# Down projections of four SwiGLU layers as seven half-size products, in an fp32 decoder trunk on one core

## What is computed

```python
D_MODEL, SEQ, DEPTH, D_FF = 1024, 512, 2, 2816

def swiglu(h, w_gate, w_up, w_down):
    return (jax.nn.silu(h @ w_gate) * (h @ w_up)) @ w_down

for i in range(DEPTH):
    f = swiglu(rmsnorm(x, ffn1_pre_norm[i]), ffn1_w_gate[i], ffn1_w_up[i], ffn1_w_down[i])
    x = x + 0.5 * rmsnorm(f, ffn1_post_norm[i])
    x = x + rmsnorm(mixer_i(rmsnorm(x, mix_pre_norm[i])), mix_post_norm[i])
    f = swiglu(rmsnorm(x, ffn2_pre_norm[i]), ffn2_w_gate[i], ffn2_w_up[i], ffn2_w_down[i])
    x = x + 0.5 * rmsnorm(f, ffn2_post_norm[i])
```

## Time and profile before

| | |
|---|---|
| median of 3 runs | 2147.71 us (2146.5 to 2147.76) |
| span of the profiled execution | 2144.4 us |
| mean granted TensorE clock | 0.999 of full speed |
| PE busy | 2134.5 us, 100% |
| DVE busy | 910.5 us, 42% |
| ACT busy | 745.2 us, 35% |
| moved by DMA | 198.20 MB, mean 92 GB/s |

### The profile page before, as it was taken

One profiled execution on the slowest core, in us unless ns is written; L12 is line 12 of the kernel. 1 busy time (PEld: TensorE's weight loads), 2 busy tenths in 40 slices (PEclk: granted clock), 3 DMA queues, 4 the chain that ended last, 5 costly groups with the idle time before them and its releaser, 6 DMA issues.

```text
span 2144.4 us, 25444 instructions
## 1 busy us (share of the span) xinstructions
PE 2134.5 (100%) x10626; PEld 1793.2 (84%) x10626; DVE 910.5 (42%) x1331; ACT 745.2 (35%) x1167; POOL 75.5 (4%) x79
## 2 busy tenths in 40 slices
PE   9999999999999999999999999999999999999998
PEld 8888888888888888888888888888897679888887
DVE  5333324476666544433322533332255555333322
ACT  5222223444545533422222332222244544222221
POOL 0000000000000000000000000000014100000000
PEclk9999999999999999999999999999999999999999
DMA  5232332222112123423233142333313113323331
GB/s 203 95 94 95 107 99 69 84 93 61 58 60 70 60 79 109 138 98 99 98 99 99 59 138 99 98 99 98 98 58 118 55 64 109 98 99 99 98 99 49
DMA packets 55828, 198.20 MB, mean 92 GB/s; under 512 B 6257, under 2 KB 6897, under 8 KB 55714
## 3 DMA queue, kind: packets, MB, share of 16 engines
q1 hardware_dynamic: 54000, 194.53, 28.3%
q10 hardware_dynamic: 1714, 2.04, 0.3%
HBM read 193.41 MB, written 2.10 MB: 91 GB/s over the span
## 4 chain that ended last, share of the span: by engine, by line
PE 96%; DVE 2%; ACT 1%; issue 1%; DMA 0%; POOL 0%; DVEq 0%; ACTq 0%; POOLq 0%
PE ps L992 18%; PE ps L994 17%; PE ps L993 17%; PE ps L1000 11%; PE ps L1002 11%; PE ps L1001 11%; PE ps L1262 1%; PE ps L1481 1%; PE ps L1510 1%; DVE w_lo L1596 1%; PE ps L1330 1%; PE ps L1019 1%; DVE normed L1602 1%; PE ps L1485 1%; PE ps L1186 1%
## 5 line engine op out<-in xcount | busy, mean ns | idle before, releaser
L992 PE MATMUL ps<-h_hi,w_hi 128*128 128x512 f32 (+1 forms) x1832 | 679.5, 371 | 0.4
L994 PE MATMUL ps<-h_hi,w_lo 128*128 128x512 f32 (+1 forms) x1832 | 674.1, 368 | 0.0
L993 PE MATMUL ps<-h_lo,w_hi 128*128 128x512 f32 (+1 forms) x1832 | 673.7, 368 | 0.0
L509 ACT ACTIVATE w_hi<-raw 128x1024 fp32r<-128x1024 f32 x352 | 370.3, 1057 | 674.0 <-PE ps L994 339.5
L1596 DVE TENSOR_TENSOR w_lo<-raw,w_hi 128x1024 fp32r<-128x1024 f32 x337 | 402.4, 1221 | 331.3 <-ACT w_hi L509 330.6
L992 PEld LDWEIGHTS ps<-h_hi,w_hi 128*128 128x128 f32 x1832 | 345.4, 189 | 59.3 <-issue 1.8
L994 PEld LDWEIGHTS ps<-h_hi,w_lo 128*128 128x128 f32 x1832 | 345.3, 188 | 58.1
L993 PEld LDWEIGHTS ps<-h_lo,w_hi 128*128 128x128 f32 x1832 | 345.5, 189 | 55.9 <-issue 0.2
L1596 DVE TENSOR_TENSOR a_rows<-a_rows,ps 128x512 f32<-128x512 f32 x88 | 60.5, 688 | 614.3 <-PE ps L994 614.3
L1000 PE MATMUL ps<-w_hi,a_hi 128*128 128x512 f32 x704 | 274.4, 390 | 0.0
L1002 PE MATMUL ps<-w_hi,a_lo 128*128 128x512 f32 x704 | 273.9, 389 | 0.0
(11 more groups left out here) (229 smaller groups left out, 1990.2 us busy)
## 6 DMA issues: line engine op xcount, KB each, us to landing
raw<-in_w_gate_up SPq DMA_DIRECT2D x176, 512.0 KB, 3.8
raw<-in_w_down SPq DMA_DIRECT2D x88, 512.0 KB, 3.6
raw<-in_w_vg SPq DMA_DIRECT2D x16, 512.0 KB, 3.6
raw<-in_w_xbc SPq DMA_DIRECT2D x16, 512.0 KB, 3.6
raw<-in_w_even_out SPq DMA_DIRECT2D x16, 512.0 KB, 4.3
raw<-in_w_qk_small SPq DMA_DIRECT2D x9, 512.0 KB, 3.7
raw<-in_w_up SPq DMA_DIRECT2D x9, 512.0 KB, 3.6
raw<-in_w_z SPq DMA_DIRECT2D x8, 512.0 KB, 3.6
```

The lines of the kernel that those rows point to most:

```text
L509: return nc.scalar.activation(to, source, ACT.Copy, scale=scale)
L992: nc.tensor.matmul(to, w_h, hi, start=first, stop=False)
L993: nc.tensor.matmul(to, w_h, lo, start=False, stop=False)
L994: return nc.tensor.matmul(to, w_l, hi, start=False, stop=last)
```

## The change

Each down projection becomes seven products of half the tokens, half the inner rows and half the columns, in the form of Strassen's algorithm with 15 additions. The inner dimension is taken in 11 pairs j of two 128-row tiles: tiles 2j and 2j+1 are the two inner halves, tokens 0 to 255 and 256 to 511 the two token halves, columns 0 to 511 and 512 to 1023 the two column halves. A slot now carries one of the seven (M1 to M7) for one or two pairs j: 42 slots with 6 groups for each M, the last group of one pair only. Each pair and each of two 128-token chunks c is one `token_products`.

- **Activations.** In the gate and up stage DVE makes per pair the four sums s1 to s4. The first three units (a11, s1, s2, for M1, M5, M6) are split on the spot into `a_split`; the other four (a22, a12, s3, s4, for M4, M2, M7, M3) go to DRAM (`spill`) and come back in the down stage (`reload`), where they are split over the first (`REFINED_AFTER`).
- **Weights.** In the gate and up stage ACT's queue loads the four quarters of the pair's down weights (1 MB, `load_job`), DVE forms four sums (`sum_weights`) and ACT's queue stores them (`store_job`). SP later loads them as slots (`load_pair`).
- **Down stage.** The order is `DOWN`; banks are collected in `update` by copies on ACT (e1) and additions on DVE (u2, v, c22, u3, c12, c21, c11), which PE waits for before it uses a bank again (`bank_free`). The steps are placed by hand at slot numbers k.
- **Boundary after a SwiGLU sublayer.** `down_stage` splits no slot of the next sublayer; two splits move into the boundary, and `add_c11` adds M2 for chunks 2 and 3.
- **Elsewhere.** `RAW` is 4.

Of the two functions `down_stage` below, the first is ACT's and the second DVE's; `down` is PE's.

```diff
-RAW = 3
+RAW = 4
...
+PAIRS = FT // 2
+GROUPS = (PAIRS + 1) // 2
+HALF_T = T // 2
...
+def plan_down():
+    order = []
+    for m in range(GROUPS):
+        order += [(name, m) for name in (("M1", "M6", "M5") if m == GROUPS - 1 else ("M6", "M5", "M1"))]
+    for m in range(GROUPS - 2):
+        order += [("M7", m), ("M3", m)]
+    order += [(name, m) for name in ("M7", "M3") for m in (GROUPS - 2, GROUPS - 1)]
+    return order + [("M4", m) for m in range(GROUPS)] + [("M2", m) for m in range(GROUPS)]
...
+BANK = {"M1": 6, "M2": 6, "M6": 2, "M7": 2, "M4": 2, "M5": 4, "M3": 4}
...
+REFINED_AFTER = [min(2 * j + 4, 23) for j in range(PAIRS)]
...
+RELOAD_AFTER = [min(2 * j, 19) for j in range(PAIRS)]
...
+            def store_job(f, j):
+                act.wait_ge(weight_sums, PAIRS * f + j + 1)
+                act.dma_start(sums[f][j], job_rows[j % 2]).then_inc(job_out[j % 2], 16)
...
+            def spill(f, j):
+                act.wait_ge(second_sums, PAIRS * f + j + 1)
+                act.dma_start(spilled[f][j], second_raw).then_inc(spill_out, 16)
...
+            def reload(f, j):
+                act.wait_ge(spill_out, 16 * (PAIRS * f + j + 1))
+                if j >= 4:
+                    act.wait_ge(second_lo, PAIRS * f + j - 3)
+                act.dma_start(back[j % 4], spilled[f][j]).then_inc(back_in[j % 4], 16)
...
+            def down_stage(f, s, n):
...
+                for k in range(C21_AFTER + 1):
+                    if k == E1_AFTER:
+                        act.wait_ge(slot_done, at + E1_AFTER + 1)
+                        for c in range(2):
+                            copy(chunk(update, 2 + c, 0), four(ps[:, BANK["M1"] + c, :])).then_inc(e1_done, 1)
...
+                    while n < stop and slot_before[n] <= at + k:
+                        split_high(n)
+                        n += 1
+                    for j in range(PAIRS):
+                        if k == REFINED_AFTER[j]:
+                            act.wait_ge(back_in[j % 4], 16 * (uses(f, j, 4) + 1))
...
+                            copy(pair(j)[:, 0:4 * HALF_T], back[j % 4]).then_inc(second_hi, 1)
+                    for j in range(PAIRS):
+                        if k == RELOAD_AFTER[j]:
+                            reload(f, j)
...
+            def down(f, s):
...
+                for k, (name, m) in enumerate(DOWN[:tail]):
+                    slot_ready(at + k)
+                    for part in range(min(2, PAIRS - 2 * m)):
...
+                        for c in range(2):
+                            if j == 0:
+                                bank_free(f, name, c)
+                            last = down_product(f, at + k, name, part, j, c)
+                    last.then_inc(slot_done, 1)
...
+            def down_stage(f, s, n):
...
+                for k in range(C21_AFTER + 1):
+                    if k == U2_AFTER:
+                        dve.wait_ge(slot_done, at + U2_AFTER + 1)
+                        for c in range(2):
+                            dve.wait_ge(e1_done, 2 * f + c + 1)
+                            add_bank(chunk(update, c, 0), chunk(update, 2 + c, 0), "M6", c, u2_done)
+                    if k == V_AFTER:
...
+                            add_bank(chunk(update, 2 + c, 1), chunk(update, c, 0), "M5", c, v_done)
...
+                    while n < stop and slot_before[n] <= at + k:
+                        split_low(n)
+                        n += 1
+                    for j in range(PAIRS):
+                        if k == REFINED_AFTER[j]:
...
+                            tt(pair(j)[:, 4 * HALF_T:8 * HALF_T], back[j % 4], pair(j)[:, 0:4 * HALF_T].bitcast(F32),
+                               ALU.subtract).then_inc(second_lo, 1)
...
                 mean_x(b, 0)
+                if b - 1 in FFN_OF:
+                    split_low(first)
                 update1(b, 1)
                 norm_x(b, 0)
                 add_update(b, 1)
                 mean_x(b, 1)
+                if b - 1 in FFN_OF:
+                    split_low(first + 1)
+                    norm_x(b, 1)
+                    add_c11(b, 2)
+                    low_of_h(b, 0)
+                    update1(b, 2)
+                    add_update(b, 2)
+                    low_of_h(b, 1)
```

More of the change, by code:

```diff
@@ L53, in plan_stages @@
 def plan_stages():
-    ffn = [[(f"gate_up{f}", 2 * FT), (f"down{f}", FT)] for f in range(N_FFN)]
+    ffn = [[(f"gate_up{f}", 2 * FT), (f"down{f}", len(DOWN))] for f in range(N_FFN)]
     groups = [stage for g in range(SG) for stage in ((f"xbc{g}", 4), (f"z{g}", 2))]
@@ L136, in plan_odd, with build_trunk @@
     return tiles, [max(b for b in used if b // 8 == slot) for slot in range(used[-1] // 8 + 1)]
-def build_trunk(nc, dram, out):
+def build_trunk(nc, dram, sums, spilled, out):
     stages, total_slots = plan_stages()
@@ L227, in squares_before, with pair @@
             return 8 + 16 * (b - 1) + NC + sum(2 if name[0] == "X" else 1 for name in at)
+        chunks_before = [sum(1 if r in FFN_OF else NC - 1 for r in range(s)) for s in range(N_SUB)]
+        def pair(j):
+            return rows(a_split, 4 * j, 4)
+        spare_rows = a_rows.rearrange("p (j r) t -> p j r t", r=4)
+        silu_rows = [rows(a_rows, 4 * b + 3) for b in range(2)]
+        job_rows = [spare_rows[:, JOB_PAIRS[b]:JOB_PAIRS[b] + 4, 3, :] for b in range(2)]
+        first_raw, second_raw = rows(extra, 0, 2), rows(extra, 2, 2)
+        back = [rows(normed, 2 * q, 2) for q in range(4)]
         def chunk(tensor, c, half):
@@ L410, in load, with load_pair @@
                 sp.dma_start(raw[n % RAW][:, :], src[:, :]).then_inc(raw_in[n % RAW], 16)
+            def load_pair(n, f, name, m):
+                if name in SUM_ROW:
+                    for j in range(2 * m, min(2 * m + 2, PAIRS)):
+                        sp.wait_ge(job_out[j % 2], 16 * (uses(f, j, 2) + 1))
+                source, row = (sums[f], SUM_ROW[name]) if name in SUM_ROW else (dram[f"w_down{f}"], WEIGHT_ROW[name])
+                count = min(2, PAIRS - 2 * m)
+                sp.wait_ge(lo_done, n - RAW + 1)
+                sp.dma_start(raw[n % RAW][:, 0:count * T].rearrange("p (j t) -> p j t", t=T),
+                             source[2 * m:2 * m + count, :, row, :].rearrange("j p t -> p j t")).then_inc(raw_in[n % RAW], 16)
             def load_x(c):
@@ L439, in _ @@
                     for n in range(RAW if first == 0 else 0, slots):
-                        load(first + n, dram["w_" + name][n])
+                        if name.startswith("down"):
+                            load_pair(first + n, FFN_OF[s], *DOWN[n])
+                        else:
+                            load(first + n, dram["w_" + name][n])
                         if first + n == (last_slot[s] + 11 if s == EVEN else first_slot[s] + 8) and s + 1 < N_SUB:
@@ L1734, in ffn @@
-                    dve.wait_ge(a_hi_ready, FT * f + tile + 1)
-                    tt(rows(a_lo, tile), rows(a_rows, FT + tile), rows(a_hi, tile).bitcast(F32), ALU.subtract).then_inc(a_lo_ready, 1)
-                out_stage(s, last_slot[s] + RING)
+                    raw_pair = second_raw if odd_tile else first_raw
+                    if not odd_tile and PAIRS * f + j:
+                        dve.wait_ge(first_lo, PAIRS * f + j)
+                    if odd_tile and PAIRS * f + j:
+                        dve.wait_ge(spill_out, 16 * (PAIRS * f + j))
```

240 lines of the change are left out of this document (208 added, 32 removed).

## The result

The changed kernel takes **2123.92 us** (median of 4 runs, 2123.54 to 2124.85) against 2147.26 for the kernel before, measured alongside: ratio 0.9892, 95% interval 0.988 to 0.9904. It is faster, by 23.3 us where 36.4 were forecast, and lies inside the range of 2096 to 2130.

A forecast was written before the change was run, and what follows sets the result against it. PE was taken to bound the kernel, busy for all of the span. Terms: -59.8 + 14.4 + 8.7 + 0.8 - 0.5 = -36.4 us, giving span 2108.0 and time 2111.3 us, range 2096 to 2130.

The forecast's parts named there:

- clock rival: Behind the seven large new stalls the granted clock falls: +9 to +18 us, time 2120 to 2129; chance 0.13.
- DMA rival: Down stage: DMA drops to about 300 GB/s, reloads are late, first stall 5.9 us: +13, time 2124; chance 0.12.
- Matmuls: Down projections: 264 fewer matmuls at 0.2267 us each, 59.8 us less, the whole gain.
- rival of another pace: Down projections: with two banks in turn matmuls take 0.245 us, costing 34 us, time 2145; chance 0.03.
- u2 and v: First stall: PE waits for DVE's additions before M7 and M3 in four sublayers, +14.4 us, bounds 0 to +26.
- The worked chain: ACT's and DVE's steps in order from slot 14: PE stands 2.7 us before M7 and 0.9 before M3.
- The boundary: Second stall: DVE's chain of 19.9 us outlasts PE's 16.7 at three boundaries after SwiGLU sublayers, net 2.9 each, +8.7 us.
- The slower rival: Down stage: each issue holds ACT until the transfer before it has landed, +59 us, time 2170; chance 0.06.
- RAW = 4: Fourth raw weight buffer returns some of PE's waits for weights around the mixers: -0.5 us.
- a doubled load fits into 10.9 us: With four raw buffers, load, both splits and hop may take 10.9 us; doubled loads need 9.5.
- The end: After the last sublayer one more addition stands behind the last matmul: +0.8 us.

The follow-up runs named there:

- e_junction: Changed kernel with u2 and v added ahead of the splits of slots 21 and 22 and three roundings of reloaded pairs later: 2111.98 us, ratio 0.9837.
- e_warm18: Changed kernel with 18 added small float32 matmuls on PE while it stands at each of three boundaries: 2120.80 us, ratio 0.9877.
- b_raw4: Kernel before the change with a fourth raw weight buffer and `dynamic_dma_scratch_size=1024`: 2147.26 us, ratio 1.0.
- e_raw3: Changed kernel with three raw weight buffers in place of four: 2147.35 us, ratio 1.0001.
- section 3: Changed kernel with small float32 matmuls added on PE at the three boundaries: 2129.82 us with 36 of them, 2120.80 us with 18.
- e_root: Changed kernel with DVE's scaling of the update moved ahead of the small sum of the two squares at the boundary: 2127.39 us, single run.

## Why the prediction was right, and where its sizes were off

The time lies in the range, and each stall stands where it was forecast. That it lies in the clock rival's band (2120 to 2129) and at the DMA rival's 2124 is in part chance: the miss is made of the boundary's size and of the clock, and no run shows a share of DMA in it.

- **Matmuls: right.** 264 fewer at 0.2267 us. The rival of another pace didn't occur: starts are 0.22 to 0.23 apart in the timeline above.
- **u2 and v: right in place and cause, too large.** +14.4 forecast, 10.5 measured in waits and 11.9 recovered by e_junction, clock included. The worked chain had 2.7 and 0.9 us; it was 2.1 and 0.7. Part of it is the reload's issue, which I let hold ACT for 0.4 us: it doesn't (next section).
- **The boundary: right in mechanism, half the size.** This is the term that failed: "It stands for 3.2 us", +8.7 with the bound at 5 per boundary, against 5.6 each, 16.8 in all, above its own bound. I took the old chain's waits as fixed (14.4 us of the earlier trace rows) and added the new work. From the first c21 at 348.56 to the end of `low_of_h(1)` at 369.99 DVE's chain in the changed kernel is 21.4 us and not 19.9. Not in the forecast are three waits of 0.44 us for POOL's root, which runs beside DVE's operations from SBUF, and 1.27 us for ACT, which squares chunk 2 before it rounds chunk 0: 2.6 us, of which other steps, shorter than I took them, gave back 1.1. The chain also starts 1.1 us after M4's last matmul, since DVE still splits a slot ahead of c21 (1.23 us at 347.42), and I had let it start at once. From M4 on that makes 22.6 us against 17.1 of work left on PE, or 5.5 of the 5.6 measured. One wait for the root comes from the order: `update1` of chunk 2 now stands right ahead of `add_update`, though the text ahead of the result says that these rows keep their old order; before, `norm_x` and `low_of_h` of other chunks stood between. And PE met the lateness twice: 1.2 us before chunk 1's transpose, which I had named only as a bound.
- **The clock: a rival with 0.13 that came true in part.** I worked out 9 to 18 us for seven stalls; it fell behind four of them, for 1.6 us in sublayer 3 and 4.7 at the boundaries (against e_warm18), less than the band had. The Trainium skill (TensorE: Matmul & The Clock Gate, "Part 1: The HAM clock gate"), by which idle brings the lower level back, was right against my "a stall of 2.7 us is short": all three stalls of 4.4 us and one of four of 2.1 brought it.
- **DMA and ACT's queue: not the bound.** The changed kernel's median landings and issues:

```profile
raw<-in_w_gate_up SPq DMA_DIRECT2D x176, 512.0 KB, 4.6
a_rows<-in_w_down ACTq DMA_DIRECT2D x44, 1024.0 KB, 9.7
sums<-a_rows ACTq DMA_DIRECT2D x44, 1024.0 KB, 7.8
raw<-sums SPq DMA_DIRECT2D x80, 512.0 KB, 5.2
```

and the issues of the reloads, from the view of that line (ns of one issue: least, median and most; first and last start in us):

```profile
L603 ACTq DMA_DIRECT2D normed<-spilled x44: 326/326/1433, 260.4 to 2061.0; - x44
```

Loads that take 3.6 us alone land in 4.6 to 5.3, where the forecast allowed 7.2, and the traffic at M7 is 316 GB/s against 289 worked out. The slower rival needed issues of over 3.1 us; the medians are 0.65 and 0.53 for the two of 1 MB and 0.33 for the two of 512 KB, and the longest of all took 1.4.
- **RAW = 4: the -0.5 was right and said too little.** b_raw4 gives 0.1. But the sentence that a doubled load fits into 10.9 us was the condition for everything else, and I had not priced its loss. e_raw3 does: 23 us, the whole gain.
- **The end:** +0.8 forecast, 1.1 measured.

The sum, on spans: the boundary's waits 8.1 too low, its clock 4.7 and the other clock loss 1.6 left out, u2 and v 3.9 too high, the end 0.3 and RAW 0.5 too low come to 11.3 of the 13.9 us missed. The other 2.6 are the small waits of section 3; what makes them up is open.

## What to carry to other kernels

When an algorithm takes work from the bound engine, work out the order of the helpers at the joints of the stages and not their mean load: here DVE was 59% busy, and two joints, the clock behind them included, took back more than half of the gain; reordering alone recovered 22 us. A chain of small steps through several engines is priced by re-reading every wait in it for what the new code does beside it, not by adding new work to the old length. And a buffer that is worth nothing before a change can be its precondition: price the cover by taking it away.

## What the runs showed of the hardware that I had not expected

- **A tiny POOL operation waits for DVE.** The root of 128 x 1 numbers takes 0.55 us, and 0.75 to 2.06 when DVE works on operands in SBUF beside it; before the change DVE read the same update from PSUM and all of them took 0.55. All 18 lengthened roots of the changed kernel's three boundaries end 0.40 to 0.42 us after an operation of DVE whose inputs both lie in SBUF, and those beside an operation that reads PSUM, or beside none, take 0.55. The Trainium skill (SBUF — State Buffer, "SBUF: two separate sides") describes a pair of ports that DVE and GpSimd share under an exclusive lock, which a DVE operation with two inputs in SBUF takes too; e_root agrees, by 0.93 to 0.55 us.
- **ACT's queue issues beside ACT's own work.** In the changed kernel's timeline an issue of 0.33 us starts inside a running activation:

```profile
298.66 1.06 ACT L577 ACTIVATE w_hi<-raw 128x1024 fp32r<-128x1024 f32 x1
298.99 0.33 ACTq L603 DMA_DIRECT2D normed<-spilled  x1
299.60 1.05 ACT L577 ACTIVATE w_hi<-raw 128x1024 fp32r<-128x1024 f32 x1
```

The next activation starts 0.94 us after the first, as two in a row do without an issue.
- **A float32 matmul of 128 columns is recorded twice and takes 0.22 us** (36 in 7.96 us), as long as one of 512 columns in fp32r.
